# Token units of a three-product float32 matmul: one interleaved pass in place of two

## The chip, the cores and the metric

The kernel runs on one core of a Trainium2 chip. TensorE (PE) multiplies, VectorE (DVE), ScalarE (ACT) and GpSimd (POOL) do elementwise work, and SyncE (SP) issues most transfers. The metric is the device time of one execution in microseconds (us); lower is better.

## The reference

The reference is a two-layer trunk over 256 tokens of width 2048, in float32. Layer 0 has two kinds of attention behind one input projection, layer 1 a gated linear recurrence; each layer then has a cross-attention into 256 memory tokens and a convolutional feed-forward part of width 5632:

```
proj = h @ w_in
...
k, v = jnp.split(memn @ wkv, [XA_W], axis=-1)
...
u = causal_depthwise_conv(h @ w_up, conv_w, conv_b)
val, gate = jnp.split(u, 2, axis=-1)
return (jax.nn.gelu(gate) * val) @ w_down
```

All weights together are some 400 MB, read once. Every large product x @ w is built from three products of rounded parts: x is split into x_hi + x_lo and w into w_hi + w_lo, all in a 32-bit format that TensorE takes in one pass, and x_hi·w_hi + x_lo·w_hi + x_hi·w_lo is summed in PSUM.

## The kernel before, in words

The weights come as a stream of 788 units of 128 x 1024 numbers (512 KB each), in the order in which they are used. For each unit SP loads `raw` (four slots, `SLOTS`), ACT writes `w_hi` from it (`split_hi`, L337), DVE writes `w_lo` = raw - w_hi (`split_lo`, L343), and TensorE multiplies. Semaphores carry it: `hi_done` and `lo_done` count the units whose high and low weights are written, `pe_unit` those that TensorE has used. ACT may write unit c only when TensorE has finished unit c - 4; SP may load unit c when DVE has read unit c - 4.

TensorE takes the units in order and in one of several helpers. 628 units have the activations as the stationary operand ("token" form, result with tokens on the partitions); 627 of them go through `token_unit`, and the very last is written out by hand (L928). They are 68 units of the input projection, 32 of the memory keys and values, 176 of each up-projection and 88 of each down-projection. A token unit holds `nk` = 2 blocks of 128 input features by 512 columns (4 units have `nk` = 4 and 256 columns), and there are two tiles of 128 tokens (`tt`), each with its own PSUM bank. So a unit is 12 matmuls: 2 blocks x 2 token tiles x 3 products. The other 160 units have the weights as the stationary operand: `pair_unit` (L370, L374), `feature_unit` (L355) and `sum_part` (L391). The last two write per block w_hi·x_hi, w_hi·x_lo, w_lo·x_hi in a row, 256 columns each.

The order on every engine is the order of the code; there is no scheduler. At the very start, unit 0 is loaded and its high part written in two halves (`hi_half`, L1040 and L1043), and the eight pairs of activation tiles of the first projection are made just ahead of their use: ACT writes x_hi (L1020), DVE x_lo (L1462), counted by `xg_l`, for which `token_unit` waits through `ready`. On DVE the order at the start is x_lo of tile 0, x_lo of tile 1, w_lo of unit 0, w_lo of unit 1. Before it, ten small matmuls on a tile of ones (L645) run.

Of the kernel before, what the change touches and what calls it, by code (L numbers as in the profile page):

```python
# [16 lines left out]
P = 128  # L17
D_MODEL, SEQ, N_MEM = 2048, 256, 256
KT = D_MODEL // P
TT = SEQ // P  # L20
# [73 lines left out]
def trunk(nc, t):  # L94
# [3 lines left out]
    with ctx:  # L98
# [11 lines left out]
        def sb(name, shape, dt=F):  # L110
            o = top[0]
            top[0] += size(shape)
            return at(name, o, shape, dt)

        def sem(name):
            return ctx.enter_context(nc.semaphore(name))
# [8 lines left out]
        w_hi = sb("w_hi", [SLOTS, UE], R)  # L125
        w_lo = sb("w_lo", [SLOTS, UE], R)
# [93 lines left out]
        ps = ctx.enter_context(nc.psum_tensor("ps", [P, 8, COLS], F))  # L220
# [4 lines left out]
        hi_done, lo_done, pe_unit = sem("hi_done"), sem("lo_done"), sem("pe_unit")  # L225

        gains_in, table_in, bias_in = sem("gains_in"), sem("table_in"), sem("bias_in")
        half_in, hi_half, ident_in = sem("half_in"), sem("hi_half"), sem("ident_in")
# [46 lines left out]
        c = 0  # L275
# [8 lines left out]
        n = 0  # L284
# [42 lines left out]
        def times(k, i, per):  # L327
            return k if i is None else k + i * per
# [67 lines left out]
        def token_unit(pe, c, k0, nk, hi, lo, bank, start, stop, ready=None, bank_free=None, i=None, per=0):  # L396

            s, n = c % SLOTS, UE // nk
            if c == 0:
                pe.wait_ge(hi_half, 1)  # L400
            else:
                pe.wait_ge(hi_done, times(c + 1, i, per))
            for k in range(nk):
                if ready:
                    ready(k0 + k)
                if c == 0 and k == 1:
                    pe.wait_ge(hi_done, 1)
                for tt in range(TT):
                    if bank_free and k == 0:
                        bank_free(tt)  # L410
                    for q, a in enumerate((hi, lo)):
                        nc.tensor.matmul(ps[:, bank + tt, 0:n], a[:, k0 + k, tt * P:tt * P + P], w_hi[:, s, k * n:k * n + n],  # L412
                                         start=start and k == 0 and q == 0, stop=False)
            pe.wait_ge(lo_done, times(c + 1, i, per))
            for k in range(nk):
                for tt in range(TT):
                    last = nc.tensor.matmul(ps[:, bank + tt, 0:n], hi[:, k0 + k, tt * P:tt * P + P], w_lo[:, s, k * n:k * n + n],  # L417
                                            start=False, stop=stop and k == nk - 1)
            last.then_inc(pe_unit, 1)


# [198 lines left out]
        def _(pe):  # L620
# [25 lines left out]
            for c, (b, u) in enumerate(TOK_UNITS):  # L646
                nk = 4 if TOK[b] == "bkv" else 2
                if u == 0 and b >= 2:

                    pe.wait_ge(tok_free, b - 1)  # L650
                token_unit(pe, c, nk * u, nk, xg_hi, xg_lo, 2 * (b % 2), u == 0, c == TOK_LAST[b],
                           (lambda k: pe.wait_ge(xg_l, k + 1)) if b == 0 else None)
                if c == STATS_AT[ATT]:
                    stats_pe(pe, ATT)
                if c == STATS_AT[MEM]:

                    pe.wait_ge(yT_done, 4)
                    stats_pe(pe, MEM)
                for nb, b2 in enumerate(NORMED):
                    if c == TURN[b2]:  # L660
                        transposes(nb)

            def mem_unit(f):
                b, u = f // U_FULL, f % U_FULL
                if f == 0:

                    pe.wait_ge(yT_done, 6)
                    pe.wait_ge(mem_lo, KT)
                token_unit(pe, first["mem"] + f, 2 * u, 2, a_hi, a_lo, 6, u == 0, u == U_FULL - 1,
                           bank_free=(lambda tt: pe.wait_ge(mem_free, TT * (b - 1) + tt + 1)) if b and u == 0 else None)  # L670
# [130 lines left out]
            def cross_attention(l):  # L801
# [71 lines left out]
                for pos, (kind, j) in enumerate(WOVEN):  # L873
                    if kind == "x" and j >= 2:
                        if j >= 4:

                            pe.wait_ge(proj_free, fblock[f"xo{l}"] + 2 + (0, 2, 4, 5)[j - 4] + 1)
                        out_part(j, range(XA_HEADS))
                    if kind == "u":
                        if j == 0:  # L880

                            pe.wait_ge(proj_free, fblock[f"xo{l}"] + 2 + 1 + 1)
                        token_unit(pe, first[f"xo{l}"] + pos, 2 * j, 2, xg_hi, xg_lo, UP_BANK[0], j == 0, j == 7, up_there)
                    if pos == 13:
                        stats_pe(pe, (FFN0, FFN1)[l])
# [1427 lines left out]
```

## Time and profile before

| | |
|---|---|
| time, median of 3 runs | 2274.31 us (2272.95 to 2274.35) |
| profiled execution, first to last instruction (span) | 2272.6 us |
| TensorE busy | 2264.1 us, 11072 matmuls |
| DVE busy | 1502.4 us |
| ACT busy | 1268.4 us |
| DMA | 455.24 MB, mean 200 GB/s |
| granted TensorE clock, mean | 0.999 |

The profiled execution is one execution; of it the profile gives the span, and no time of its own beside it. Busy times are unions of what an engine's instructions cover. A matmul's own duration (some 390 ns for 512 columns) is modelled and overlaps the next, so the rate is read from start to start, not from the duration. The profile numbers lines as in the listing above.

### The profile page before, as it was taken

Reading aid. Unit: us, or ns where it says so; the run is one execution under the profiler, and the core shown is the slowest. Engines: PE = TensorE matmul, PEld = TensorE weight load, DVE = VectorE, ACT = ScalarE, POOL = GpSimd, SP = SyncE. Lnnn points to the kernel's source line nnn. Section 1 sums busy time; section 2 is a strip of 40 time slices with the busy share of each in tenths; the row PEclk is TensorE's granted clock in tenths of the full one; section 3 lists DMA queues with packets and bytes.
Section 4 is the critical chain, followed back from the end, with each engine's and each line's share of the span. In section 5 each row is a group of like instructions: output and inputs, shape, how many; then the busy total and the mean of one; then the engine's idle time right before and its main releaser. Section 6 shows DMA issues by size and latency. Waiting matters only on the chain.

```text
span 2272.6 us, 33897 instructions
## 1 busy us (share of the span) xinstructions
PE 2264.1 (100%) x11072; PEld 1911.0 (84%) x11072; DVE 1502.4 (66%) x1812; ACT 1268.4 (56%) x1663; POOL 619.1 (27%) x1027
## 2 busy tenths in 40 slices
PE   9999999999999999999999999999999999999999
PEld 7888888988888888888888888898888888888887
DVE  6766775676767667665556778658767767665443
ACT  6655664565556555544444777556655655554333
POOL 0720001234343343412221100215434344340000
PEclk9999999999999999999999999999999999999999
DMA  8655435547776776766665555636867676776555
GB/s 274 207 199 200 133 126 176 176 151 219 217 223 214 222 222 213 222 206 202 203 203 188 174 193 175 200 126 216 253 220 221 216 223 212 221 221 193 194 193 167
DMA packets 143779, 455.24 MB, mean 200 GB/s; under 512 B 25888, under 2 KB 26784, under 8 KB 143696
## 3 DMA queue, kind: packets, MB, share of 16 engines
q1 hardware_dynamic: 117696, 420.40, 58.0%
q0 software_dynamic: 25856, 33.65, 4.9%
q8 instruction: 54, 0.88, 0.2%
q14 instruction: 29, 0.24, 0.0%
q10 hardware_dynamic: 144, 0.06, 0.0%
HBM read 423.73 MB, written 2.10 MB: 187 GB/s over the span
## 4 chain that ended last, share of the span: by engine, by line
PE 99%; ACT 0%; DVE 0%; DMA 0%; issue 0%; SPq 0%; ACTq 0%
PE ps L412 50%; PE ps L417 25%; PE ps L370 10%; PE ps L374 5%; PE ps L355 2%; PE ps L391 2%; PE ps L729 1%; PE ps L978 1%; PE ps L715 0%; PE ps L809 0%; PE ps L698 0%; PE ps L637 0%; DMA xT<-in_x_t 0%; PE ps L691 0%; PE ps L830 0%
## 5 line engine op out<-in xcount | busy, mean ns | idle before, releaser
L343 DVE TENSOR_TENSOR w_lo<-raw,w_hi 128x1024 fp32r<-128x1024 f32 x788 | 978.8, 1245 | 702.4 <-ACT w_hi L337 699.6
L337 ACT ACTIVATE w_hi<-raw 128x1024 fp32r<-128x1024 f32 x787 | 830.8, 1059 | 855.7 <-PE ps L417 738.7
L412 PE MATMUL ps<-w_hi,xg_hl 128*128 128x512 f32 (+1 forms) x3392 | 832.9, 388 | 1.9 <-DVE xg_hl L1462 1.9
L412 PEld LDWEIGHTS ps<-w_hi,xg_hl 128*128 128x128 f32 x3392 | 631.8, 188 | 131.4 <-DVE xg_hl L1462 2.4
L417 PE MATMUL ps<-w_lo,xg_hl 128*128 128x512 f32 (+1 forms) x1696 | 450.1, 388 | 0.0
L412 PE MATMUL ps<-w_hi,a_hl 128*128 128x512 f32 x1656 | 411.9, 391 | 0.3 <-ACT vmem L1110 0.2
L417 PEld LDWEIGHTS ps<-w_lo,xg_hl 128*128 128x128 f32 x1696 | 317.0, 188 | 65.3
L412 PEld LDWEIGHTS ps<-w_hi,a_hl 128*128 128x128 f32 x1656 | 308.8, 188 | 65.0 <-issue 0.7
L2140 POOL DMA_DIRECT2D u_t<-z_t x704 | 346.5, 500 | 2.8 <-issue 2.8
L417 PE MATMUL ps<-w_lo,a_hl 128*128 128x512 f32 x828 | 221.4, 389 | 0.0
L417 PEld LDWEIGHTS ps<-w_lo,a_hl 128*128 128x128 f32 x828 | 155.4, 188 | 32.5
L370 PE MATMUL ps<-xg_hl,w_hi 128*128 128x512 f32 x512 | 161.7, 397 | 0.0
L1814 DVE SCALAR_TENSOR_TENSOR y_iter<-u_t,fconv,y_iter 128x256 f32 (+1 forms) x352 | 146.6, 480 | 0.3
L2137 POOL TENSOR_TENSOR sq<-ones 128x1 f32<-128x1 f32 x44 | 26.2, 596 | 385.3 <-DVE z_t L1801 385.3
L374 PEld LDWEIGHTS ps<-xg_hl,w_lo 128*128 128x128 f32 x512 | 96.2, 188 | 22.7
L374 PE MATMUL ps<-xg_hl,w_lo 128*128 128x256 f32 x512 | 100.6, 278 | 0.0
L1290 ACT ACTIVATE y_iter<-u_t,fconv 128x256 f32 (+1 forms) x176 | 94.9, 587 | 0.5 <-DMA u_t<-z_t 0.5
L370 PE MATMUL ps<-o_hl,w_hi 128*128 128x512 f32 x256 | 80.5, 396 | 0.1
L370 PE MATMUL ps<-a_hl,w_hi 128*128 128x512 f32 x256 | 80.4, 395 | 0.0
L370 PEld LDWEIGHTS ps<-xg_hl,w_hi 128*128 128x128 f32 x512 | 78.3, 189 | 0.3
L2146 POOL TENSOR_TENSOR u_t<-u_t,ones 128x24 f32<-128x24 f32 x44 | 18.6, 423 | 174.3 <-DMA u_t<-z_t 174.3
L1462 DVE SCALAR_TENSOR_TENSOR xg_hl<-xT,gains,xg_hl 128x256 fp32r<-128x256 f32 (+1 forms) x96 | 58.7, 659 | 7.5 <-ACT xg_hl L1020 7.5
(215 smaller groups left out, 1779.2 us busy)
## 6 DMA issues: line engine op xcount, KB each, us to landing
raw<-in_w_stream SPq DMA_DIRECT2D x787, 512.0 KB, 4.2
u_t<-z_t POOLq DMA_DIRECT2D x704, 34.0 KB, 3.4
bias<-in_rel_bias POOLq DMA_DIRECT2D x4, 768.0 KB, 5.8
memT<-in_mem_t POOLq DMA_DIRECT2D x4, 512.0 KB, 6.0
gate_w<-in_gate_w POOLq DMA_DIRECT2D x4, 512.0 KB, 3.8
x_tok<-x_turned SPq DMA_DIRECT2D x16, 128.0 KB, 4.3
out_t<-x_tok SPq DMA_DIRECT2D x8, 256.0 KB, 4.3
u_dn<-z_dn POOLq DMA_DIRECT2D x48, 32.0 KB, 3.2
```

Of the source, the lines that this page charges most:

```text
L337: nc.scalar.activation(w_hi[:, s, :], raw[:, s, :], ACT.Copy).then_inc(hi_done, 1)
L343: nc.vector.tensor_tensor(w_lo[:, s, :], raw[:, s, :], w_hi[:, s, :].bitcast(F), ALU.subtract).then_inc(lo_done, 1)
L355: last = nc.tensor.matmul(ps[:, bank, 0:SEQ], a[:, s, w], b[:, k0 + k, :], start=start and k == 0 and q == 0, stop=stop and k == nk - 1 an ...
L370: nc.tensor.matmul(ps[:, bank + m, :], w_hi[:, s, w], both, start=start and k == ks[0], stop=False, skip_group_check=True)
L374: last = nc.tensor.matmul(ps[:, bank + m, SEQ:2 * SEQ], w_lo[:, s, w], x[:, xk, 0, :], start=False, stop=stop and k == ks[-1], skip_group_ ...
L391: last = nc.tensor.matmul(ps[:, bank + m, 0:SEQ], a[:, s, w], x[:, k, b, :], start=k == 0 and q == 0, stop=k == XA_HEADS - 1 and q == 2)
L412: nc.tensor.matmul(ps[:, bank + tt, 0:n], a[:, k0 + k, tt * P:tt * P + P], w_hi[:, s, k * n:k * n + n], start=start and k == 0 and q == 0, ...
L417: last = nc.tensor.matmul(ps[:, bank + tt, 0:n], hi[:, k0 + k, tt * P:tt * P + P], w_lo[:, s, k * n:k * n + n], start=False, stop=stop and ...
L1290: A(chunks(y_tile(half, m - 4 * back, i)), u_t[:, :, m, HALO:RUN], ACT.Identity, scale=column(fconv, w + 2, i, 32), bias=column(fconv, w + ...
L1462: V.scalar_tensor_tensor(dst, src, gain, hi.bitcast(F), ALU.mult, ALU.subtract).then_inc(count, 1)
L1814: V.scalar_tensor_tensor(y, u_t[:, :, m, HALO - 2 + j:RUN - 2 + j], column(fconv, 4 * (4 * (1 - half) + m) - 32 * back + j, i, 32), y, ALU ...
L2140: pool.dma_start(u_t[SQ * b:SQ * b + SQ, a, :, :].rearrange("p k n -> p (k n)"), z_t[SQ * a:SQ * a + SQ, b, :, :].rearrange("p k n -> p (k ...
```

## The change

The two passes of `token_unit` become one. Before, all products with `w_hi` of the unit came first (x_hi·w_hi and x_lo·w_hi for each block and token tile), then, behind a wait for `lo_done`, all products with `w_lo`. Now each block and token tile has its three products in a row: x_hi·w_hi, x_hi·w_lo, x_lo·w_hi. The wait for `hi_done` is gone, and the one for `lo_done` stands ahead of the unit. Unit 0's start on its half-written high part (`hi_half`) is gone too.

```
-            if c == 0:
-                pe.wait_ge(hi_half, 1)
-            else:
-                pe.wait_ge(hi_done, times(c + 1, i, per))
+            pe.wait_ge(lo_done, times(c + 1, i, per))
             for k in range(nk):
                 if ready:
                     ready(k0 + k)
-                if c == 0 and k == 1:
-                    pe.wait_ge(hi_done, 1)
                 for tt in range(TT):
                     if bank_free and k == 0:
                         bank_free(tt)
-                    for q, a in enumerate((hi, lo)):
-                        nc.tensor.matmul(ps[:, bank + tt, 0:n], a[:, k0 + k, tt * P:tt * P + P], w_hi[:, s, k * n:k * n + n],
-                                         start=start and k == 0 and q == 0, stop=False)
-            pe.wait_ge(lo_done, times(c + 1, i, per))
-            for k in range(nk):
-                for tt in range(TT):
-                    last = nc.tensor.matmul(ps[:, bank + tt, 0:n], hi[:, k0 + k, tt * P:tt * P + P], w_lo[:, s, k * n:k * n + n],
-                                            start=False, stop=stop and k == nk - 1)
+                    for q, (a, w) in enumerate(((hi, w_hi), (hi, w_lo), (lo, w_hi))):
+                        last = nc.tensor.matmul(ps[:, bank + tt, 0:n], a[:, k0 + k, tt * P:tt * P + P], w[:, s, k * n:k * n + n],
+                                         start=start and k == 0 and q == 0, stop=stop and k == nk - 1 and q == 2)
             last.then_inc(pe_unit, 1)
```

TensorE at the start of the program, units 0 and 1 (`xg_hl` holds x_hi and x_lo, the stationary operand; the rows do not tell which). Before:

```order
L412 MATMUL ps<-w_hi,xg_hl 128x512 [waits xg_l,hi_half]
L412 MATMUL ps<-w_hi,xg_hl 128x512 x3
L412 MATMUL ps<-w_hi,xg_hl 128x512 [waits hi_done,xg_l]
L412 MATMUL ps<-w_hi,xg_hl 128x512 x3
L417 MATMUL ps<-w_lo,xg_hl 128x512 [waits lo_done]
L417 MATMUL ps<-w_lo,xg_hl 128x512 x3
L412 MATMUL ps<-w_hi,xg_hl 128x512 [waits hi_done]
L412 MATMUL ps<-w_hi,xg_hl 128x512 x7
```

And of the change:

```order
L407 MATMUL ps<-w_hi,xg_hl 128x512 [waits xg_l,lo_done]
L407 MATMUL ps<-w_lo,xg_hl 128x512
L407 MATMUL ps<-w_hi,xg_hl 128x512 x2
L407 MATMUL ps<-w_lo,xg_hl 128x512
L407 MATMUL ps<-w_hi,xg_hl 128x512
L407 MATMUL ps<-w_hi,xg_hl 128x512 [waits xg_l]
L407 MATMUL ps<-w_lo,xg_hl 128x512
L407 MATMUL ps<-w_hi,xg_hl 128x512 x2
```

The first matmul of unit 0 waited for half of the high weights and now waits for all of the low ones; the second block's wait for the activations comes after six matmuls, not four.

TensorE in the loop of an up-projection, at the head of its body (`up_out` tells that the banks are free). Before:

```order
L402 ISA [waits up_out]
L412 MATMUL ps<-w_hi,xg_hl 128x512 [waits hi_done]
L412 MATMUL ps<-w_hi,xg_hl 128x512 x7
L417 MATMUL ps<-w_lo,xg_hl 128x512 [waits lo_done]
L417 MATMUL ps<-w_lo,xg_hl 128x512 x3
L402 REGISTER_ALU
L412 MATMUL ps<-w_hi,xg_hl 128x512 [waits hi_done]
```

And of the change:

```order
L399 ISA [waits up_out]
L407 MATMUL ps<-w_hi,xg_hl 128x512 [waits lo_done]
L407 MATMUL ps<-w_lo,xg_hl 128x512
L407 MATMUL ps<-w_hi,xg_hl 128x512 x2
L407 MATMUL ps<-w_lo,xg_hl 128x512
L407 MATMUL ps<-w_hi,xg_hl 128x512 x2
L407 MATMUL ps<-w_lo,xg_hl 128x512
L407 MATMUL ps<-w_hi,xg_hl 128x512 x2
L407 MATMUL ps<-w_lo,xg_hl 128x512
L407 MATMUL ps<-w_hi,xg_hl 128x512
L399 REGISTER_ALU
```

The unit still has twelve matmuls; a `w_lo` one now stands between every two with `w_hi`, and the unit has one wait, at its head. Nothing moves on the other engines.

## Rows read from the trace of the kernel before

**Rows 1.** The page: busy time by engine, and the chain's shares by line.

```profile
PE 2264.1 (100%) x11072; PEld 1911.0 (84%) x11072; DVE 1502.4 (66%) x1812; ACT 1268.4 (56%) x1663; POOL 619.1 (27%) x1027
...
PE ps L412 50%; PE ps L417 25%; PE ps L370 10%; PE ps L374 5%; PE ps L355 2%; PE ps L391 2%; PE ps L729 1%; PE ps L978 1%; PE ps L715 0%; PE ps L809 0%; PE ps L698 0%; PE ps L637 0%; DMA xT<-in_x_t 0%; PE ps L691 0%; PE ps L830 0%
```

**Rows 2.** Waits: who waited for whom, us in total, times, longest.

```profile
PE ps L412 <- DVE xg_hl L1462: 1.9, 1, 1.9
...
ACT w_hi L337 <- PE ps L417: 738.7, 527, 4.0
```

**Rows 3.** Timeline of PE in down-projection 0: start us, us, what, count.

```profile
1001.76 1.98 PE L412 MATMUL ps<-w_hi,a_hl 128*128 128x512 f32 x8
...
1004.48 1.98 PE L412 MATMUL ps<-w_hi,a_hl 128*128 128x512 f32 x8
```

**Rows 4.** Groups by line and shape: busy us, mean ns of one, idle before.

```profile
L412 PE MATMUL ps<-w_hi,xg_hl 128*128 128x512 f32 x3328 | 824.6, 390 | 1.9 <-DVE xg_hl L1462 1.9
...
L412 PEld LDWEIGHTS ps<-w_hi,xg_hl 128*128 128x128 f32 x3392 | 631.8, 188 | 131.4 <-DVE xg_hl L1462 2.4 <-ACT w_hi L1040 0.2
...
L355 PEld LDWEIGHTS ps<-xg_hl,w_hi 128*128 128x128 f32 x256 | 39.8, 192 | 0.0
```

**Rows 5.** Timeline of PE in the last unit, L928.

```profile
2266.57 0.62 PE L928 MATMUL ps<-w_hi,a_hl 128*128 128x512 f32 x2
2267.02 0.39 PE L928 MATMUL ps<-w_lo,a_hl 128*128 128x512 f32 x1
...
2269.06 0.39 PE L928 MATMUL ps<-w_lo,a_hl 128*128 128x512 f32 x1
```

**Rows 6.** Timeline of PE in a feature unit, L355.

```profile
432.20 0.40 PE L355 MATMUL ps<-xg_hl,w_hi 128*128 128x256 f32 x2
...
433.64 0.40 PE L355 MATMUL ps<-xg_hl,w_hi 128*128 128x256 f32 x2
```

**Rows 7.** Timeline of PE in a pair unit, L370 and L374.

```profile
349.62 0.63 PE L370 MATMUL ps<-o_hl,w_hi 128*128 128x512 f32 x2
350.09 0.39 PE L374 MATMUL ps<-o_hl,w_lo 128*128 128x256 f32 x2
350.32 0.63 PE L370 MATMUL ps<-o_hl,w_hi 128*128 128x512 f32 x2
```

**Rows 8.** Timeline of the start, PE and DVE, units 0 to 2.

```profile
5.77 1.17 PE L412 MATMUL ps<-w_hi,xg_hl 128*128 128x512 f32 x4
...
8.26 0.48 DVE L1462 SCALAR_TENSOR_TENSOR xg_hl<-xT,gains,xg_hl 128x256 fp32r<-128x256 f32 x1 [2.63 <-ACT xg_hl L1020]
8.78 2.48 DVE L343 TENSOR_TENSOR w_lo<-raw,w_hi 128x1024 fp32r<-128x1024 f32 x2
...
8.89 1.82 PE L412 MATMUL ps<-w_hi,xg_hl 128*128 128x512 f32 x4 [1.95 <-DVE xg_hl L1462]
...
10.51 1.91 PE L417 MATMUL ps<-w_lo,xg_hl 128*128 128x512 f32 x4
...
12.21 2.18 PE L412 MATMUL ps<-w_hi,xg_hl 128*128 128x512 f32 x8
...
15.15 1.98 PE L412 MATMUL ps<-w_hi,xg_hl 128*128 128x512 f32 x8
```

**Rows 9.** Windows of the start: us, busy by engine, PEclk, DMA share, GB/s.

```profile
8.90:12.30 3.40, 3.40 (x9) 2.64 (x10) 3.12 (x4) 2.57 (x4) 0.00 (x0) 0.54 1.03 407
12.30:20.00 7.70, 7.70 (x35) 6.34 (x34) 4.89 (x6) 4.88 (x8) 0.00 (x0) 0.98 0.99 377
```

**Rows 10.** L343 alone from 0 to 1552.26 us: DVE busy, how many.

```profile
0.00:1552.26 1552.26, 657.42 (x526) 1.00 0.61 195
```

**Rows 11.** Timeline: w_lo and the units they serve, two places.

```profile
1551.02 1.23 DVE L343 TENSOR_TENSOR w_lo<-raw,w_hi 128x1024 fp32r<-128x1024 f32 x1 [0.54 <-ACT w_hi L337]
...
1553.23 1.09 PE L412 MATMUL ps<-w_hi,xg_hl 128*128 128x512 f32 x4
...
2259.76 1.23 DVE L343 TENSOR_TENSOR w_lo<-raw,w_hi 128x1024 fp32r<-128x1024 f32 x1 [1.50 <-ACT w_hi L337]
```

## Prediction

> **What bounds the kernel now.** I read the page first. TensorE covers practically the whole span, and the chain that ended last is TensorE's, three quarters of it in the two lines that the change merges, L412 and L417 [rows 1]. A chain like that can still hide waits, so the list of waits comes next: TensorE's longest is 1.9 us, once, for the activations of tile 1 at the start, while ACT stands 738.7 us before its splits until TensorE frees a slot [rows 2]. The other engines wait for TensorE; TensorE waits for nobody. In such a kernel two things alone move the time: how long one matmul takes from start to start, and what TensorE idles at the start.
>
> The rate is read from starts. In a down-projection one unit begins at 1001.76 and the next at 1004.48 [rows 3]: 2.72 us for 12 matmuls, 226.7 ns each. At 2.4 GHz 512 columns take 213.3 ns, so 13.3 ns of each step are something else. There are 3328 matmuls of this shape with `xg_hl` in L412 alone, and each has its own weight load: L412 has as many loads as matmuls over both its shapes [rows 4]. In all 7572 matmuls go through `token_unit`: 623 units of 12 and 4 of 24.
>
> **The change, part by part.** It removes no matmul, no load and no split. It changes the order, and one wait.
>
> *The step.* Since 7572 steps are concerned, 0.6 ns on each would be 4.5 us, 0.2% of the time, about what a measurement of this kernel can tell from no change. So the question is whether three products in a row run at another step. The new order has three kinds of neighbours. From x_hi·w_hi to x_hi·w_lo the stationary tile is the same and the moving block another. From x_hi·w_lo to x_lo·w_hi both change. From there to the next token tile or block both or one change. Three places of this trace have such neighbours.
> - The last unit is written out with w_hi, w_hi, w_lo for each block, both blocks of a token tile in a row, so six matmuls into one bank. Its twelve start at 2266.57 to 2269.06 [rows 5]: 11 steps in 2.49 us, 226.4 ns. Interleaving w_lo with w_hi, and six into one bank, cost and give nothing there. Its stationary tiles differ from one matmul to the next, though, and it is only twelve matmuls long.
> - The feature units (L355) have w_hi twice as the stationary operand, then w_lo. From 432.20 to 433.64 there are four rounds of three [rows 6], 1.44 us for 12 steps, 120.0 ns. 256 columns at 2.4 GHz are 106.7 ns; again 13.3 ns beside them, the same as in the token units. If a stationary tile that is already there saved anything, one step in three would be shorter and the mean below that. The load is also still made: L355 has 256 loads of w_hi for 256 matmuls [rows 4]. 128 of them load what is there.
> - The pair units (L370, L374) show that the step is not a constant: two matmuls of 512 columns take 0.47 us from 349.62 to 350.09, 235 ns each, and two of 256 take 0.23, 115 ns each [rows 7]. An order can shift a step by some 6 to 8 ns.
>
> No place has the same stationary tile twice with 512 columns. Bounds: below, the whole 13.3 ns falls away where the tile stays; above, a step takes the 233 to 235 ns of the pair unit. Of the two nearest rows both say 13.3 ns as now, so I cost the step at nothing and keep both ends for the rivals.
>
> The Trainium skill ("TensorE: Matmul & The Clock Gate", Part 2, What happens when you issue a matmul) says that weights are loaded by an instruction of their own so that one load can serve many matmuls, and gives a back-to-back gap of columns / 2.4 GHz plus about 2.5 ns. By it a token step would be 215.8 ns, not 226.7, and an order that keeps the tile could save up to 11 ns at each of 2524 places, 27 us. The trace has 13.3 ns beside the columns in every steady step and a load for each matmul.
>
> *The wait for `lo_done` moves from two thirds of the unit to its head*, 8 steps or 1.8 us earlier. Where would the low weights be late? At the end of the program the last w_lo (unit 787) is written by 2259.76 + 1.23 = 2260.99 [rows 11], and its unit begins at 2266.57 [rows 5]: 5.6 us early. I looked for the tightest place behind the start: the first up-projection unit of a woven stretch, unit 525, begins at 1553.23; 526 low parts (units 0 to 525) had begun by 1552.26 [rows 10], the last of them at 1551.02, ended at 1552.25 [rows 11]. That is 0.98 us before the unit's first matmul, where the wait now stands. So no unit but 0 waits, and the price is nothing. If that cover went (DVE's split 1 us later) the loss would be what it is late by, per place. `pe_unit` still comes at the unit's end, so ACT, DVE and SP are released as before. Queued behind this wait on TensorE is only the unit itself.
>
> *Unit 0.* Here it costs. Before, four matmuls ran from 5.77, on half of the high weights; the next four began at 8.89, when x_lo of tile 1 was there, the four with w_lo at 10.51, unit 1 at 12.21 and unit 2 at 15.15 [rows 8]. DVE writes w_lo of units 0 and 1 in 2.48 us from 8.78, so that of unit 0 is done at 10.02. TensorE started 0.15 us behind DVE's end at tile 1 (8.26 + 0.48 = 8.74 to 8.89); so all twelve now start at 10.17.
>
> From then the clock decides. Between 8.9 and 12.3 the granted clock is 0.54, afterwards 0.98 of full over 7.7 us [rows 9]: the lower level, 1.2 GHz, until about 12.5, and steps of (12.21 - 10.51) / 4 = 0.427 us. Before it fell TensorE had stood idle for some 2 us; it rose when TensorE had been busy since 8.89. Now the idle time ahead is longer (some 4 us behind the ten small matmuls), and it falls no later. Count to the start of unit 2, 24 steps:
> - Clock back at the same moment, 12.5: 5.5 steps of 0.427, 18.5 of 0.227, so unit 2 at 16.7, 1.6 us late.
> - Clock back as long after the first matmul as before (3.7 us, at 13.9): 8.7 slow steps, 15.3 others, unit 2 at 17.3, 2.2 us late.
> - All of unit 0 slow and two steps more: 14 slow, 10 others, 18.4, 3.3 us late.
>
> I take the middle, 2.2 us. ACT's and DVE's next splits wait for data at that time, not for TensorE, so nothing stretches this; and nothing makes it up, since TensorE is the bound from there to the end.
>
> *Small things.* The second block's wait for activations comes after six matmuls in place of four, which can only ease; no such wait is left to ease behind unit 0. One semaphore less per unit costs or gives nothing that a row shows.
>
> **Sum.** 0 for 7572 steps, 0 for 626 waits, +2.2 us for unit 0. Against the profiled span that is 2272.6 + 2.2 = 2274.8; the median of the runs stands 1.7 us above the span, so 2276.5 us.
>
> **Rivals.**
> - *The tile that stays saves its 13.3 ns* (faster). 2524 steps have the same stationary tile as the one before (four per unit, eight in the four wide ones); 2524 x 13.3 ns = 33.6 us, less 2.2: 2243. For it: the gap that the profile does not explain. Against it: L355 with its repeated tile, at the same 13.3 ns, and its undiminished loads. Chance 8%. One such step per unit would give 627 x 13.3 = 8 us: 2268, another 3%.
> - *The new order falls into the pair units' step* (slower). All steps at 233 ns, 6.3 more: 48 us, 2324. For it: [rows 7]; against it: the last unit, L355. It decides from 0.3 ns per step on, since 2.2 us are lost already and 4.5 are the bound. 6%. Only some steps: one in twelve 4 us, a third 16 us (2280 to 2292), 9%.
> - *The low weights are late* (slower): they must come 1 us later than now at the tightest places, or some 4 us later in the loops; 1 to 5 us in all, 2279. 3%.
> - *As forecast*, the start alone: 2275 to 2279. 71%.
>
> **Numbers.** The forecast's own range is 2275.0 to 2278.5 and holds some 7 in 10. To hold 8 in 10 the range takes in one changed step of twelve on the fast side (2268 to 2276, cut at 2270) and one to two on the slow side (to 2285). Faster by over 0.2% (under 2269.8): 8% and 3%. Slower by over 0.2% (over 2278.9): 6, 9 and most of 3, and 1 from a start that costs more, 18%. The rest, 71%, is within 0.2%.
>
> **What would show it.** In the timeline of the loops a unit still takes 2.72 us, now from one line, L407. The groups show 7572 matmuls in it and as many loads. The timeline of the start has TensorE idle until about 10.2 and unit 2 at about 17.3. No wait for w_lo appears but at unit 0. The forecast is wrong if the unit's length moves by more than 7 ns (0.6 on each of 12 steps); the timeline of one loop shows that at once.

## The result, and the profile after

| | before | after |
|---|---|---|
| time, median of 19 runs | 2272.66 us (2271.87 to 2274.35) | 2276.41 us (2274.61 to 2277.88, and one at 2287.70) |
| ratio, 95% interval | | 1.0017 (1.0011 to 1.0024) |
| span of the profiled execution | 2272.6 us | 2274.7 us |

The change costs 3.75 us, 0.17%. That is inside 0.2%, yet the interval does not touch 1: it is a small loss. With 19 runs the median of before is 2272.66, not the 2274.31 of the three runs that the forecast started from. The time of an execution is 1.7 to 1.9 us more than its span in every run here, so the execution of before whose profile was read took some 2274.4: it was one of the two slowest of the 19 (2274.35 and 2274.31). Why that matters comes below.

First the page of after, to be laid beside [rows 1], busy time by engine:

```profile
PE 2264.4 (100%) x11072; PEld 1912.0 (84%) x11072; DVE 1502.7 (66%) x1812; ACT 1268.9 (56%) x1663; POOL 619.8 (27%) x1027
```

The counts are the same, and TensorE is busy 0.3 us longer while the span is 2.1 us longer. The rest is idle time: the wait that came (3.7) less the wait that went (1.9). The list of waits (who waited for whom: us, times, longest) has it in its first row:

```profile
PE ps L407 <- DVE w_lo L343: 3.7, 1, 3.7
...
ACT w_hi L337 <- PE ps L407: 739.2, 529, 4.0
```

TensorE waits for low weights once in the whole program, 3.7 us; the wait of 1.9 us for tile 1 [rows 2] is not in the list any more. ACT's idle time before its splits is what it was. Where the one wait lies, the timeline of the start shows:

```profile
7.38 0.48 DVE L1452 SCALAR_TENSOR_TENSOR xg_hl<-xT,gains,xg_hl 128x256 fp32r<-128x256 f32 x1 [1.70 <-ACT xg_hl L1010]
7.90 1.23 DVE L343 TENSOR_TENSOR w_lo<-raw,w_hi 128x1024 fp32r<-128x1024 f32 x1
...
9.18 0.79 PE L407 MATMUL ps<-w_hi,xg_hl 128*128 128x512 f32 x1 [3.74 <-DVE w_lo L343]
...
10.19 1.05 PE L407 MATMUL ps<-w_hi,xg_hl 128*128 128x512 f32 x2
...
14.89 0.48 PE L407 MATMUL ps<-w_lo,xg_hl 128*128 128x512 f32 x1
...
17.29 0.62 PE L407 MATMUL ps<-w_hi,xg_hl 128*128 128x512 f32 x2
```

Unit 0 starts when its low weights end (7.90 + 1.23 = 9.13) and not at 5.77 [rows 8]. From 10.19 to 14.89 there are 11 steps, 0.427 us each, the lower clock level. The last row covers the end of unit 1 and the first matmul of unit 2, which starts a step behind 17.29, at 17.51; before it was 15.15. The clock by windows (us, busy by engine, PEclk, DMA share, GB/s) says the same; in [rows 9] the second window had 0.98:

```profile
8.90:12.30 3.40, 3.12 (x7) 2.48 (x8) 2.33 (x4) 2.22 (x4) 0.00 (x0) 0.50 1.01 402
12.30:20.00 7.70, 7.70 (x29) 6.20 (x28) 5.28 (x6) 5.21 (x9) 0.00 (x0) 0.82 1.03 411
```

And the loops. In the same down-projection as [rows 3] one row in three is a `w_lo` matmul:

```profile
1001.40 0.39 PE L407 MATMUL ps<-w_lo,a_hl 128*128 128x512 f32 x1
1001.63 0.62 PE L407 MATMUL ps<-w_hi,a_hl 128*128 128x512 f32 x2
...
1004.12 0.39 PE L407 MATMUL ps<-w_lo,a_hl 128*128 128x512 f32 x1
```

Four triples, 12 steps, take 1004.12 - 1001.40 = 2.72 us, as before. The trace has 7572 matmuls in L407 and 7572 loads. The place that the prediction took as the tightest for the moved wait, unit 525, now stands like this:

```profile
1553.14 1.23 DVE L343 TENSOR_TENSOR w_lo<-raw,w_hi 128x1024 fp32r<-128x1024 f32 x1 [0.54 <-ACT w_hi L337]
...
1555.36 0.40 PE L407 MATMUL ps<-w_hi,xg_hl 128*128 128x512 f32 x1
```

Its low weights end at 1554.37, 0.99 us ahead of its first matmul, the margin of before [rows 10, 11] moved by 2.1 us. (Unit 2 starts 2.36 us later than before, unit 525 2.13 us: some 0.2 us of the lateness was made up on the way, where the prediction had said that nothing would.)

### The profile page after: what moved, and what is told of

It is laid out like the page before. It is cut to its first block, busy times and chain, and to the rows that moved or that the text cites. A ratio compares the mean times of both kernels' runs of the same rounds, so it can differ in the third digit from the quotient of the medians.

```text
span 2274.7 us, 33896 instructions
## 1 busy us (share of the span) xinstructions
PE 2264.4 (100%) x11072; PEld 1912.0 (84%) x11072; DVE 1502.7 (66%) x1812; ACT 1268.9 (56%) x1663; POOL 619.8 (27%) x1027
## 4 chain that ended last, share of the span: by engine, by line
PE 99%; ACT 0%; DVE 0%; issue 0%; DMA 0%; SPq 0%; ACTq 0%
PE ps L407 75%; PE ps L370 10%; PE ps L374 5%; PE ps L355 2%; PE ps L391 2%; PE ps L719 1%; PE ps L968 1%; PE ps L705 0%; PE ps L799 0%; PE ps L688 0%; PE ps L627 0%; PE ps L681 0%; PE ps L820 0%; DMA xT<-in_x_t 0%; DVE w_lo L343 0%
## 5 line engine op out<-in xcount | busy, mean ns | idle before, releaser
L343 DVE TENSOR_TENSOR w_lo<-raw,w_hi 128x1024 fp32r<-128x1024 f32 x788 | 978.9, 1245 | 704.4 <-ACT w_hi L337 701.7
L407 PE MATMUL ps<-w_hi,xg_hl 128*128 128x512 f32 (+1 forms) x3392 | 1043.2, 388 | 3.7 <-DVE w_lo L343 3.7
L407 PEld LDWEIGHTS ps<-w_hi,xg_hl 128*128 128x128 f32 x3392 | 636.1, 188 | 133.8 <-DVE w_lo L343 3.9
L407 PE MATMUL ps<-w_lo,xg_hl 128*128 128x512 f32 (+1 forms) x1696 | 657.8, 388 | 0.0
L407 PE MATMUL ps<-w_hi,a_hl 128*128 128x512 f32 x1656 | 516.9, 391 | 0.3 <-ACT vmem L1100 0.2
L407 PEld LDWEIGHTS ps<-w_lo,xg_hl 128*128 128x128 f32 x1696 | 319.3, 188 | 64.5
L407 PEld LDWEIGHTS ps<-w_hi,a_hl 128*128 128x128 f32 x1656 | 310.9, 188 | 65.5 <-issue 0.7
L407 PE MATMUL ps<-w_lo,a_hl 128*128 128x512 f32 x828 | 322.3, 389 | 0.0
L407 PEld LDWEIGHTS ps<-w_lo,a_hl 128*128 128x128 f32 x828 | 155.5, 188 | 31.5
L370 PE MATMUL ps<-xg_hl,w_hi 128*128 128x512 f32 x512 | 161.8, 397 | 0.0
L374 PEld LDWEIGHTS ps<-xg_hl,w_lo 128*128 128x128 f32 x512 | 96.2, 188 | 22.7
L374 PE MATMUL ps<-xg_hl,w_lo 128*128 128x256 f32 x512 | 100.7, 278 | 0.0
L370 PE MATMUL ps<-o_hl,w_hi 128*128 128x512 f32 x256 | 80.5, 396 | 0.1
L370 PE MATMUL ps<-a_hl,w_hi 128*128 128x512 f32 x256 | 80.4, 395 | 0.0
L370 PEld LDWEIGHTS ps<-xg_hl,w_hi 128*128 128x128 f32 x512 | 78.3, 189 | 0.3
L2109 POOL TENSOR_TENSOR acc<-acc,x_sq_out 128x256 f32<-128x256 f32 x16 | 14.4, 903 | 179.5 <-ACT x_sq_out L1188 179.5
```

Source lines behind the costliest of these rows:

```text
L343: nc.vector.tensor_tensor(w_lo[:, s, :], raw[:, s, :], w_hi[:, s, :].bitcast(F), ALU.subtract).then_inc(lo_done, 1)
L370: nc.tensor.matmul(ps[:, bank + m, :], w_hi[:, s, w], both, start=start and k == ks[0], stop=False, skip_group_check=True)
L374: last = nc.tensor.matmul(ps[:, bank + m, SEQ:2 * SEQ], w_lo[:, s, w], x[:, xk, 0, :], start=False, stop=stop and k == ks[-1], skip_group_ ...
L407: last = nc.tensor.matmul(ps[:, bank + tt, 0:n], a[:, k0 + k, tt * P:tt * P + P], w[:, s, k * n:k * n + n], start=start and k == 0 and q = ...
```

## Experiments

Each kernel was timed beside the kernel before on the same chip: 11 runs of it against 15 to 33 of the kernel before where a ratio is given, one run of it otherwise. "The change" below is the kernel after. The intervals of the ratios are some 2 us wide to either side; where a difference below is smaller than that, the single runs are compared.

**1. Is all of the loss in unit 0?** Two kernels cut the change in two. The first has the change but for unit 0, which keeps its two passes of before:

```
+            if c == 0:
+                pe.wait_ge(hi_half, 1)
...
+                return
             pe.wait_ge(lo_done, times(c + 1, i, per))
```

> The change everywhere but in unit 0, which has its two passes and its early start on half of the high weights again. If the loss is all in unit 0 (my theory: order and moved waits cost nothing elsewhere), this stands at the time of the kernel before, ratio 1.0000 with the interval over it, and unit 2 starts at about 15.2 us. If part of the loss is spread over the other units (the median lost 3.7 us, the profiled spans only 2.1), some 1.5 us stay, ratio 1.0007.

Measured: 2272.87 against 2272.80, ratio 1.0001 (0.9992 to 1.0010). Its timeline of PE at the start:

```profile
5.81 1.16 PE L407 MATMUL ps<-w_hi,xg_hl 128*128 128x512 f32 x4 [0.59 <-DVE xg_hl L1469]
7.61 1.15 PE L407 MATMUL ps<-w_hi,xg_hl 128*128 128x512 f32 x4 [0.63 <-DVE xg_hl L1469]
8.78 1.20 PE L412 MATMUL ps<-w_lo,xg_hl 128*128 128x512 f32 x4
10.69 0.50 PE L424 MATMUL ps<-w_hi,xg_hl 128*128 128x512 f32 x1 [0.72 <-DVE w_lo L343]
...
13.34 0.63 PE L424 MATMUL ps<-w_hi,xg_hl 128*128 128x512 f32 x2
```

Four matmuls cover 1.2 us, at the upper clock level; where they run at the lower one, four cover 1.9 (10.51 in [rows 8]).

Two things differ from what was expected. Unit 2 (the second matmul of the last row) starts at 13.57 and not at 15.2: this execution has no slow steps, the profiled one of before had. And unit 1 waits 0.72 us for its low weights. So the moved wait does have a place of its own behind unit 0; in the change, unit 0's late start hides it. What it costs here is not to be read from the medians, which lie 0.07 us apart: the interval would hide 0.7 us.

The second is the kernel before with unit 0's wait alone changed:

```
             if c == 0:
-                pe.wait_ge(hi_half, 1)
+                pe.wait_ge(lo_done, 1)
...
-                if c == 0 and k == 1:
-                    pe.wait_ge(hi_done, 1)
```

> The kernel before with one wait changed: unit 0 waits for all of its low weights at its head, in two passes as before. If unit 0's start is the whole loss, this has all of it: ratio 1.0015 to 1.0017, 3.3 to 3.8 us over the kernel before, unit 2 at 17.3 to 18.4 us. If the order of the matmuls carries part of it, it is less: about 2 us, 1.0009.

Measured: 2276.64 against 2272.80, ratio 1.0015 (1.0006 to 1.0024), 3.84 us. A loss of the size of the change's, 3.75, is there with two passes everywhere; and with one pass in 626 units and the old start it is gone. Its waits and its timeline read like those of the change:

```profile
PE ps L410 <- DVE w_lo L343: 3.7, 1, 3.7
```

```profile
9.58 3.78 PE L410 MATMUL ps<-w_hi,xg_hl 128*128 128x512 f32 x8 [3.72 <-DVE w_lo L343]
13.16 1.55 PE L415 MATMUL ps<-w_lo,xg_hl 128*128 128x512 f32 x4
14.55 2.01 PE L410 MATMUL ps<-w_hi,xg_hl 128*128 128x512 f32 x8
```

8 steps from 9.58 to 13.16 are 0.45 us each, near the 0.427 of the lower level. The mean granted clock of this execution reads 1.0 all the same, as in 4 more of its 11 runs, so the steps are the surer sign.

**2. Is a repeated stationary tile worth anything?** The change with the products in another order, so that no tile stands twice:

```
-for q, (a, w) in enumerate(((hi, w_hi), (hi, w_lo), (lo, w_hi))):
+for q, (a, w) in enumerate(((hi, w_hi), (lo, w_hi), (hi, w_lo))):
```

> The change with the three products in the order x_hi w_hi, x_lo w_hi, x_hi w_lo: no stationary tile stands twice in a row. If a tile that is already there saves nothing and costs nothing (my theory), a loop unit takes 2.72 us and the time is that of the change, ratio 1.0017 to the kernel before. If a repeated tile saved part of the 13.3 ns that some other effect gave back, this one would be slower by up to 2524 x 13.3 ns = 34 us.

Measured: 2276.41 against 2272.80, ratio 1.0015 (1.0006 to 1.0024), the same median as the change to the hundredth. And the other way, one tile three times:

```
+for q, (a, w) in enumerate(((hi, w_hi), (hi, w_lo), (hi, w_hi))):
```

> The change with x_hi in place of x_lo in the third product, so that for each block and token tile one stationary tile serves three matmuls in a row (the small part x_lo w_hi of the result is left out). If a tile that is already there saves nothing, a loop unit takes 2.72 us, the span is 2274 to 2276. If it saves its 13.3 ns, two steps of three are shorter: 2.61 us per unit, 67 us less.

Measured: one run, 2276.19, span 2274.4. In its timeline, the down-projection:

```profile
1001.05 0.39 PE L407 MATMUL ps<-w_lo,a_hl 128*128 128x512 f32 x1
...
1003.77 0.39 PE L407 MATMUL ps<-w_lo,a_hl 128*128 128x512 f32 x1
```

2.72 us for 12 steps; the same two rows stand in the timeline of the kernel with no repeat. Repeated never, once in three or twice in three: 226.7 ns.

**3. How much of the loss is the clock?** The change with TensorE kept busy until unit 0 (each small matmul on ones makes two records in the trace):

```
-for _ in range(10):
+for _ in range(26):
     nc.tensor.matmul(ps[:, 7, 0:P], ones[:, :], ones[:, :], start=True, stop=True)
```

> The change with 26 in place of 10 small matmuls on ones ahead of unit 0, so that TensorE is busy until about 9.1 us. If the loss is mostly the low clock (13 steps of 0.427 in place of 0.227, 2.6 us) that follows the idle time, the clock stays at its upper level and unit 2 starts at 14.7 to 15.7 us; the time is then within 1 us of the kernel before, ratio 0.9997 to 1.0004. If the loss is the late start by itself, it stays at 1.0015.

Measured: 2274.26 against 2272.80, ratio 1.0007 (0.9998 to 1.0016). The timeline of PE, and above it DVE's row for the low weights of units 0 and 1:

```profile
8.30 2.54 DVE L343 TENSOR_TENSOR w_lo<-raw,w_hi 128x1024 fp32r<-128x1024 f32 x2
5.01 4.57 PE L635 MATMUL ps<-ones 128*128 128x128 f32 x35
9.58 0.50 PE L407 MATMUL ps<-w_hi,xg_hl 128*128 128x512 f32 x1
...
12.67 0.39 PE L407 MATMUL ps<-w_lo,xg_hl 128*128 128x512 f32 x1
...
14.71 0.39 PE L407 MATMUL ps<-w_lo,xg_hl 128*128 128x512 f32 x1
14.94 0.62 PE L407 MATMUL ps<-w_hi,xg_hl 128*128 128x512 f32 x2
```

The clock stays up: 9 steps in 2.04 us. The small matmuls held up nothing: they end at 9.58, the low weights at about 9.5. Neither of the two expectations holds alone. By the medians the 3.75 us split into 1.5 that stay, the late start, and 2.2 that go, the low clock. The interval of this ratio touches both 1.0000 and 1.0015, but the single runs lie apart: these 11 between 2273.87 and 2274.89, 26 of the 33 of before beside them at 2273.54 or less, 18 of the 19 of the change at 2275.02 or more. The profiles give about the same parts. Unit 2 starts at 13.57 in the first kernel of experiment 1, at 15.17 here (the second matmul of the last row) and at 17.51 in the change: 1.6 us, then 2.3.

**4. Can the kernel before be helped in the same way?** It has a gap of its own in unit 0. Eight small matmuls go there in a first kernel, and in a second that has the interleaved loops of experiment 1 too; in a third kernel four:

```
             for k in range(nk):
+                if c == 0 and k == 1:
+                    for _ in range(8):
+                        nc.tensor.matmul(ps[:, 7, 0:P], ones[:, :], ones[:, :], start=True, stop=True)
                 if ready:
```

> The kernel before with 8 small matmuls on ones between the first and the second block of unit 0, into the idle 2 us there (0.22 us each at the upper clock). If the low clock from 8.9 to 12.5 us follows from that idle time, it goes, and 9 to 10 steps of 0.427 become 0.227: 1.8 us less, ratio 0.9992. If the clock falls anyway, no difference, or up to 0.5 us more where the small matmuls reach past the arrival of the data.

> The change in all units but 0, unit 0 as before, and the 8 small matmuls in its gap. Order and waits costing nothing, it stands with the kernel before plus the same small matmuls: ratio 0.9992. If the interleaved order helps or harms by itself, it differs from that by what it is worth.

> The kernel before with 4 small matmuls on ones (0.9 us at the upper clock) in the idle gap of unit 0. With 8 of them the clock stayed up in all 11 runs, but these stood 0.4 us above the executions of the kernel before whose clock stayed up too. If 4 still keep the clock up and end before the data is there, the median is 2272.4 to 2272.8 with none near 2274: ratio 0.9995 to 1.0000. If they are too few, about one execution in five still lies near 2274 and nothing is gained.

Measured: eight, 2273.09 against 2272.89, ratio 1.0002 (0.9993 to 1.0011); eight with the interleaved loops of experiment 1, 2273.26 against 2272.89, 1.0001 (0.9992 to 1.0010); four, 2272.82 against 2272.80, 1.0000 (0.9991 to 1.0009). No gain in any median, and the 1.8 us that the first two expectations named did not come. The timeline of the first:

```profile
8.27 0.48 DVE L1465 SCALAR_TENSOR_TENSOR xg_hl<-xT,gains,xg_hl 128x256 fp32r<-128x256 f32 x1 [2.67 <-ACT xg_hl L1023]
7.31 1.95 PE L406 MATMUL ps<-ones 128*128 128x128 f32 x16
9.01 1.17 PE L415 MATMUL ps<-w_hi,xg_hl 128*128 128x512 f32 x4
10.07 1.19 PE L420 MATMUL ps<-w_lo,xg_hl 128*128 128x512 f32 x4
11.10 1.99 PE L415 MATMUL ps<-w_hi,xg_hl 128*128 128x512 f32 x8
```

In this profile tile 1 is as late as in that of before (8.27 and 8.26), and the clock stays up: no four matmuls behind 9.01 cover 1.9 us, and unit 1 starts at 11.10, not 12.21. But it mends what seldom breaks. Of the kernel before, 12 of the 15 runs beside the four have a mean clock of 1.000 and 2272.09 to 2273.10 us, and 3 have 0.999 and 2274.35 to 2274.63. The median lies in the first kind, and there the small matmuls are not missed. Whether they take the second kind away isn't shown. All 33 runs with small matmuls read 1.000, but that reading is no sure sign (experiment 1), and by the times 4 of the 33 lie above 2273.9, one of them (2274.04) with four, where the expectation had none near 2274; of the 36 runs of before beside them 7 do. With eight the next block starts 0.26 us behind the end of tile 1 (8.75 to 9.01), where it was 0.15: they reach a little past the data.

**5. What is in a step?** Two kernels make one product in three unlike its neighbours.

```
-last = nc.tensor.matmul(ps[:, bank + tt, 0:n], a[:, k0 + k, tt * P:tt * P + P], w[:, s, k * n:k * n + n],
+m = P // 2 if q == 1 else P
+last = nc.tensor.matmul(ps[0:m, bank + tt, 0:n], a[:, k0 + k, tt * P:tt * P + m], w[:, s, k * n:k * n + n],
```

> The change with the second product, x_hi w_lo, for the first 64 of each 128 tokens alone: its stationary tile has 64 columns, so one load of three is half as long (that part of the result is left out for the other tokens). If the 13.3 ns per step are the load's (it sets the step, or part of it), those steps shrink and the unit goes from 2.72 to 2.67 us or less. If the load lies wholly under the matmul before it, as the rate of the two forms of 256 and 512 columns suggests, nothing changes: 2.72.

Measured: one run, 2298.82, span 2297.0: 22.3 us longer than the change, with less to load. Its groups and its timeline:

```profile
L408 PEld LDWEIGHTS ps<-w_lo,xg_hl 128*64 128x64 f32 x1696 | 228.2, 135 | 70.1
```

```profile
1001.42 0.40 PE L408 MATMUL ps<-w_lo,a_hl 128*64 128x512 f32 x1
1001.65 0.62 PE L408 MATMUL ps<-w_hi,a_hl 128*128 128x512 f32 x2
...
1004.17 0.40 PE L408 MATMUL ps<-w_lo,a_hl 128*64 128x512 f32 x1
```

Those loads take 135 ns, not 188, and twelve steps take 2.75 us, not 2.72: 229 to 230 ns each. Over 7572 steps some 3 ns make the 22 us. Both expectations were wrong: the unit neither got shorter nor stayed the same. It is not the narrow matmul alone that takes longer. Taken over all the starts in this trace, a step from one full-width matmul to another full-width one is 230.0 ns in the mean, where it is 226.9 in the change. The edit halves the rows written in PSUM along with the load, and no run has narrow loads alone, so which of the two does it isn't shown.

The other shortens the moving side of the same product:

```
+e = n // 2 if q == 1 else n
+last = nc.tensor.matmul(ps[:, bank + tt, 0:e], a[:, k0 + k, tt * P:tt * P + P], w[:, s, k * n:k * n + e],
```

> The change with the second product, x_hi w_lo, for the first 256 of the 512 columns alone (that part of the result is left out). If each step depends on its own matmul alone, a unit takes 8 x 226.7 + 4 x 120 ns = 2.29 us. If a mix of lengths disturbs the neighbours, as a mix of load widths did (2.76 in place of 2.72 us), the steps of 512 columns lie at 231 to 236 ns as in the pair units.

Measured: one run, 2205.98, span 2204.2. Timeline in an up-projection:

```profile
900.25 0.28 PE L408 MATMUL ps<-w_lo,xg_hl 128*128 128x256 f32 x1
900.38 0.63 PE L408 MATMUL ps<-w_hi,xg_hl 128*128 128x512 f32 x2
900.84 0.28 PE L408 MATMUL ps<-w_lo,xg_hl 128*128 128x256 f32 x1
...
903.19 0.28 PE L408 MATMUL ps<-w_lo,xg_hl 128*128 128x256 f32 x1
```

Five triples take 2.94 us, 588 ns each, where 2 x 226.7 + 120 would be 573. So this mix of lengths disturbs too. The pair units are no second case of it. In the trace of before, the fifth row of theirs like the first of [rows 7] is:

```profile
352.40 0.63 PE L370 MATMUL ps<-o_hl,w_hi 128*128 128x512 f32 x2
```

Four rounds from 349.62 to 352.40 are 695 ns each, where 2 x 226.7 + 2 x 120 is 693: what their long steps take more, their short ones take less. A unit of the shortened kernel is 2.35 us and not 2.72, which would be 232 us over 627 units, but the span fell by 70.5. The page, the waits and a window tell most of why:

```profile
PE 2079.5 (94%) x11072; PEld 1763.7 (80%) x11072; DVE 1498.2 (68%) x1812; ACT 1248.5 (57%) x1663; POOL 617.5 (28%) x1027
```

```profile
PE ps L408 <- DVE w_lo L343: 101.8, 73, 3.6
```

```profile
600.00:800.00 200.00, 176.41 (x859) 143.79 (x858) 133.11 (x170) 108.76 (x136) 78.01 (x162) 0.99 0.67 214
```

TensorE is busy 176 us of the 200 in that window. In the whole program it is idle 124.7 us (2204.2 - 2079.5), of which 101.8 are 73 waits for low weights, and its mean granted clock is 0.988, so part of its matmuls run slower as well. A TensorE that needs 14% less per unit meets the splits and what feeds them.

## Why the prediction was right, and where it was off

- *The step costs nothing.* Right: 2.72 us per unit after, and with a repeated stationary tile in none, one or two of three places (experiment 2). The rival of a saved load (2243 us) is refuted. No stream of these three-product matmuls steps, over a whole round, at less than some 13 ns beside its columns. The Trainium skill ("TensorE: Matmul & The Clock Gate", Part 2, What happens when you issue a matmul) has 2.5 ns there; the measurement decides.
- *The moved wait costs nothing in 626 units.* Right for the change: one wait in the list, 0.99 us of margin at unit 525, and experiment 1 at 1.0001. The reason given, that the low weights are early everywhere, has one gap: unit 1 is covered by unit 0's lateness, and with the old start it waited 0.72 us (experiment 1).
- *Unit 0 costs 2.2 us.* Right in place and mechanism, too small as a term: the medians say 3.75, and experiment 1 finds a loss of that size there and none clear of noise elsewhere. Two things in that term were off.
  - Its base. The term compared with the profiled start of before, which had a low-clock stretch of its own from 8.9 to 12.5 us. Most executions of before take some 1.7 us less than that one (the median is 2272.66, that one took some 2274.4) and read a mean clock of 1.000 (experiment 4), and the start profiled in the first kernel of experiment 1, which has unit 0 as before, has no slow steps. Against such a start the slow steps of unit 0 are all loss, 2.2 us, beside 1.5 of lateness (experiment 3). Between the two profiled executions the difference is 2.1 us, and that was the difference that the sum had costed, at 2.2.
  - Its clock. The middle case was taken, back up at 13.9 us with 8.7 slow steps; in the profile it was nearly the third (14 slow steps): 13 slow steps, up at about 15.0. The data happened to come 0.9 us earlier than in the profile of before (tile 1, which DVE makes ahead of w_lo, was done at 7.86, not 8.74), which offset it, so unit 2 stood at 17.51 where 17.3 was forecast.
- *The time, 2276.5 us.* Measured 2276.41. That they agree to 0.1 us is luck. Two errors cancel: the loss was 1.5 us too small and the base, a median of three runs with two near 2274.3, 1.65 us too high.
- *The slower rival, the pair units' step.* It did not come. Its price of 233 ns was half of a reading: in those units the steps of 512 columns are 6 to 8 ns longer and those of 256 columns 5 ns shorter, and a round takes 695 ns where the uniform rates give 693. That is a mix of lengths, not an order; no order of like matmuls that was run shifted the step (experiment 2). Unlike neighbours can lengthen a stream, though: experiment 5 has two cases, one of 22 us. The change keeps all shapes alike.

## What to carry to other kernels

Reordering like matmuls in this stream, bound by TensorE, was worth nothing by itself in any of three orders. Look at what a reordering does to the first unit, where nothing is buffered yet. A one-time start cost is measured against the usual start: compare several executions before taking one profile as the base, since a stretch of low clock at the start comes and goes. Do not count on a gain from a shorter load: here the stream became slower by it.

## What the runs showed of the hardware that was not expected

- A shorter load made the stream slower: one load in three at 64 columns (135 ns in place of 188) took the mean step from 226.7 to some 229.5 ns, and steps between two full-width matmuls with it.
- One matmul in three with 256 columns: 588 ns per three, 14 more than its parts at their own uniform rates. The pair units, two of 512 and two of 256 in turn, take 235 and 115 ns and in sum nearly what the uniform rates give. What in the engine does this stays open; these runs show that it came with unlike neighbours, in load or in length, and with no order of like ones.
- The 13.3 ns beside the columns of each step in a uniform stream (226.7 at 512, 120.0 at 256) stayed with every order tried. What they are was not found.
- The low clock at the start went with TensorE's idle time: with 1.95 us ahead of 8.89 [rows 8] and with 3.74 ahead of 9.18 in the change it fell; in the first kernel of experiment 1, whose tile came earlier, gaps of 0.6 us ahead of 5.81 and 7.61 did not bring it down, and where small matmuls filled the idle time (experiments 3 and 4) the profiles have no slow steps either.
